# Split fp32r products for q, k and all inputs of the state-space stage in a two-block transformer kernel

## The reference, cut to what matters

```python
proj = x @ w_in                                   # retention: q, k, v, g
q, k, v, g = jnp.split(proj, [RET_QK_W, 2 * RET_QK_W, 2 * RET_QK_W + RET_V_W], axis=-1)
...
prj_c = modulate(rmsnorm(ctx, norm1[layer]), sh1c, sc1c) @ w_in[layer]   # second block: context
prj_l = modulate(rmsnorm(x, norm1[layer]), sh1, sc1) @ w_in[layer]       # second block: tokens
z_c, xbc_c, dt_c, f_c = split_proj(prj_c)
z_l, xbc_l, dt_l, f_l = split_proj(prj_l)
```

## Time and profile before

| what | value |
|---|---|
| time, median of 3 runs | 1798.87 us (1797.41 to 1799.01) |
| span of the profiled execution | 1797.4 us |
| TensorE busy | 1699.7 us (95%) |
| VectorE, ScalarE busy | 642.6 us (36%), 510.6 us (28%) |
| q and k on TensorE | 111.1 to 167.0 us |
| state-space inputs on TensorE | 944.6 to 1096.3 us |

### The profile page before, as it was taken

The page is one execution under the profiler, slowest core; times in us unless marked ns, Lnnn a source line. Parts: engine busy times, 40 slices in busy tenths (PEclk is TensorE's granted clock), DMA queues, the critical chain, the costliest instruction groups (busy, mean ns, idle before and its releaser), DMA issues.

```text
span 1797.4 us, 22709 instructions
## 1 busy us (share of the span) xinstructions
PE 1699.7 (95%) x9752; PEld 1308.8 (73%) x9752; DVE 642.6 (36%) x1038; ACT 510.6 (28%) x751; POOL 5.1 (0%) x13
## 2 busy tenths in 40 slices
PE   6999999999999999999989997869699999999996
PEld 6988899999999989999974476548444545454543
DVE  4434214554365504555323462740321212121212
ACT  5420024444444404444332222430201110111011
POOL 0000000000000000000000000000000000000000
PEclk9999898999899696999969998999799999999999
DMA  9552334555455533555532131002099999999992
GB/s 391 188 187 94 141 141 162 185 186 185 174 190 188 186 140 141 188 188 188 188 140 94 47 141 53 1 4 94 33 396 420 425 416 425 419 424 418 424 419 100
DMA packets 26988, 382.94 MB, mean 213 GB/s; under 512 B 3056, under 2 KB 3184, under 8 KB 3360
## 3 DMA queue, kind: packets, MB, share of 16 engines
q1 hardware_dynamic: 26208, 377.71, 53.7%
q0 software_dynamic: 704, 4.11, 0.6%
HBM read 380.76 MB, written 1.05 MB: 212 GB/s over the span
## 4 chain that ended last, share of the span: by engine, by line
PE 92%; DVE 3%; ACT 3%; issue 1%; DMA 0%; DVEq 0%; ACTq 0%; SPq 0%
PE ps L427 83%; PE ps L770 4%; PE ps L779 4%; DVE HM L1151 1%; ACT HM L839 1%; DVE HM L1139 1%; PE ps L505 1%; ACT work L839 1%; ACT L839 0%; DVE work L1139 0%; PE ps L818 0%; PE ps L812 0%; DMA X<-in_x 0%; ACT SQ L839 0%; DVE work L1151 0%
## 5 line engine op out<-in xcount | busy, mean ns | idle before, releaser
L427 PE MATMUL ps<-ring,work 128*64 128x512 f32 x1536 | 336.9, 595 | 12.3 <-ACT work L839 12.3
L427 PEld LDWEIGHTS ps<-ring,work 128*64 128x64 f32 x1536 | 107.5, 137 | 221.9 <-issue 207.1
L1139 DVE TENSOR_TENSOR w_lo<-ring,w_hi 128x1024 fp32r<-128x1024 f32 x156 | 190.8, 1225 | 191.7 <-ACT w_hi L839 191.2
L427 PE MATMUL ps<-in_hi,w_hi 128*128 128x256 f32 x896 | 256.1, 286 | 0.0
L427 PE MATMUL ps<-in_lo,w_hi 128*128 128x256 f32 x896 | 255.5, 285 | 0.0
L427 PE MATMUL ps<-in_hi,w_lo 128*128 128x256 f32 x896 | 255.2, 285 | 0.0
L839 ACT ACTIVATE work<-ps 128x512 f32<-128x512 f32 (+2 forms) x148 | 87.6, 626 | 575.9 <-PE ps L427 328.9
L839 ACT ACTIVATE w_hi<-ring 128x1024 fp32r<-128x1024 f32 x156 | 164.8, 1058 | 204.5 <-PE ps L427 204.5
L427 PE MATMUL ps<-HM,ring 128*128 128x256 f32 (+1 forms) x704 | 197.7, 441 | 6.8 <-ACT HM L839 6.8
L427 PEld LDWEIGHTS ps<-HM,ring 128*128 128x128 f32 x704 | 133.9, 192 | 63.8 <-issue 49.9
L427 PEld LDWEIGHTS ps<-in_hi,w_hi 128*128 128x128 f32 x896 | 173.1, 193 | 0.0
(11 more groups left out here) (180 smaller groups left out, 1744.6 us busy)
## 6 DMA issues: line engine op xcount, KB each, us to landing
ring<-in_experts SPq DMA_DIRECT2D x96, 2048.0 KB, 12.2
ring<-in_dense SPq DMA_DIRECT2D x83, 2048.0 KB, 8.1
cst<-in_ret_cst POOLq DMA_DIRECT2D x1, 1280.0 KB, 12.8
X<-in_x SPq DMA_DIRECT2D x1, 1024.0 KB, 5.5
cst<-in_ssd_cst POOLq DMA_DIRECT2D x1, 1024.0 KB, 5.0
work<-in_ctx POOLq DMA_DIRECT2D x1, 1024.0 KB, 9.5
out<-HM SPq DMA_DIRECT2D x1, 1024.0 KB, 3.9
cst<-in_wfour POOLq DMA_DIRECT2D x1, 256.0 KB, 2.9
```

The lines of the kernel that those rows point to most:

```text
L427: i = pe.matmul(o, l, r, start=start, stop=stop)
L1139: i = dve.tensor_tensor(out=o, in0=x, in1=y, op=op)
```

## The change

q and k, and all inputs of the state-space stage, become split products with three fp32r passes. dt's weights and the inputs `hcat` are split too (`wdt_hi`, `wdt_lo`, `cat_hi`, `cat_lo`). The 5.5 units of these weights are 44 chunks more, 16 for q and k and 28 for xs, b, c, z and f, which ScalarE copies and VectorE subtracts. To make room, dense units use five slots of the ring, and four in the state-space stage: slot 5 holds two of the three pairs of chunk buffers, slot 4 `cat_hi`. In the state-space stage the third pair lies in `cst`, so that `ssd_cst` is loaded behind f. The experts take the slots in another order.

```diff
+DENSE_SLOTS, SSD_SLOTS = 5, 4
+SLOT = [u % DENSE_SLOTS if u < UNIT_AT["ssd_xs", 0] else (u - UNIT_AT["ssd_xs", 0]) % SSD_SLOTS for u in range(DENSE)]
+TURN = [SLOT[:u].count(SLOT[u]) for u in range(DENSE)]
+EXPERT_SLOT = [2, 4, 5, 3, 0, 1]
...
-        w_at = [("cst", 0), ("work", 2 * KF * T), ("HM", 0)]
+        w_at = [("ring5", 0), ("ring5", 2 * CHUNK), ("HM", 0)]
...
         def chunks_by(name, j):
+            if name == "ssd_in":
+                return min(CHUNK_AT["ssd_xs"][0] + j + 3, CHUNK_AT["ssd_z"][0] + 2)
...
             await_read(pool, TILE["ffn_out1", 3])
+            pool.dma_start(ctxT, a["ctx"]).then_inc(s["ld_ctx"], 16)
+            await_full(pool, TILE["ssd_f", 1])
             pool.dma_start(cst[:, 0:2048], a["ssd_cst"]).then_inc(s["ld_ssd"], 16)
-            pool.dma_start(ctxT, a["ctx"]).then_inc(s["ld_ctx"], 16)
...
-            gemm("ret_q", "q", 8, KD, lambda c: H[:, c, :])
-            gemm("ret_k", "k", 8, KD, lambda c: H[:, c, :])
+            split_gemm("ret_q", KD, KD, in_hi, in_lo, tile="q")
+            split_gemm("ret_k", KD, KD, in_hi, in_lo, tile="k")
...
+            def cat_ready(c):
+                pe.wait_ge(s["cat_lo_ready"], KD + c + 1)
+
             for m in range(KX + KB):
                 name, i = ("ssd_xs", m) if m < KX else ("ssd_b", m - KX)
-                gemm(name, "ssd_in", 1, KD, lambda c: hcat[:, c, :],
-                     (lambda c: pe.wait_ge(s["h_ready"], KD * 5 + c + 1)) if m == 0 else None, cols=2 * T, per=1,
-                     first_block=i * KD, first_tile=m)
+                split_gemm(name, 1, KD, cat_hi, cat_lo, cat_ready if m == 0 else None, tile="ssd_in", per=1, cols=2 * T,
+                           first_tile=m, first_block=i * KD)
...
-            gemm("ssd_z", "ssd_z", KX, KD, lambda c: hcat[:, c, T:2 * T])
-            gemm("ssd_f", "ssd_f", FG, KD, lambda c: hcat[:, c, T:2 * T])
+            split_gemm("ssd_z", KX, KD, lat_hi, lat_lo)
+            split_gemm("ssd_f", FG, KD, lat_hi, lat_lo)
...
+            weights_hi(CHUNK_AT["ffn_in0"][0])
             for j in range(2 * HEADS):
...
             modulated(0, lambda c: hcat[:, c, 0:T], lambda c: coef[:, 0, c:c + 1], lambda c: mod[:, c, 1:2])
+            cat_split(0, 0)
             modulated(1, lambda c: hcat[:, c, T:2 * T], lambda c: coef[:, 1, c:c + 1], lambda c: mod[:, c, 0:1])
+            cat_split(1, T)
+            act.wait_ge(s["ld_wdt"], 16)
+            fn(wdt_hi[:, :, :], wdt[:, :, :], ACT.Copy, s["wdt_hi_ready"])
...
-            weights_lo(CHUNK_AT["ffn_in0"][0])
+            weights_lo(CHUNK_AT["ret_q"][0])
...
             for kind, dst in (("q", q), ("k", k)):
                 for h in range(HEADS):
                     t = TILE[kind, h]
+                    weights_lo(chunks_by(f"ret_{kind}", h))
                     await_full(dve, t)
...
             dve.wait_ge(s["dt_act"], 3)
+            weights_lo(z_chunk + 3)
             log1p_end(dtb, dtc, dta, dtx, scr)
+            weights_lo(z_chunk + 6)
```

More of the change, by code:

```diff
@@ L390, in _ @@
                 with sp.Fori(1, n_rounds) as r:
-                    expert_round(r)
+                    for n in range(RING):
+                        early = 1 if n >= RING - 2 else 0
+                        sp.wait_ge(slot_used[EXPERT_SLOT[n]], r * (EXPERT_UNITS // RING) + (DENSE_USES[EXPERT_SLOT[n]] + early))
+                        load_expert(n, n)
+                    expert_rest(r * (EXPERT_UNITS // RING))
             sp.wait_ge(s["h_ready"], KD * 9)
@@ L869, in inv_rms, with cat_split @@
                 fn(rstd_of(n), lnb[:, :], ACT.Exp, s["rstd_ready"], scale=-0.5)
+            def cat_split(k, lo):
+                for c in range(KD):
+                    act.wait_ge(s["h_ready"], KD * (4 + k) + c + 1)
+                    fn(cat_hi[:, c, lo:lo + T], hcat[:, c, lo:lo + T], ACT.Copy, s["cat_hi_ready"])
             def modulated(k, dst, gain, shift):
@@ L1033, in _ @@
             for m in range(KX + KB):
+                weights_hi(chunks_by("ssd_in", m))
                 padded(m)
@@ L1039, in _ @@
             for m in range(KB):
+                weights_hi(chunks_by("ssd_in", KX + KB + m))
                 padded(KX + KB + m)
@@ L1044, in _ @@
             silu_tile(KX + 2 * KB - 1)
+            weights_hi(CHUNK_AT["ssd_z"][0] + 3)
             act.wait_ge(s["dt_dve"], 1)
@@ L1053, in _ @@
             for j in range(4):
+                weights_hi(chunks_by("ssd_z", j))
                 read(TILE["ssd_z", j], pairs(mix, j), ACT.Silu)
             for j in range(2):
+                weights_hi(chunks_by("ssd_f", j))
                 read(TILE["ssd_f", j], pairs(mix, 4 + j))
@@ L1340, in _ @@
             settle(tt(mod[:, :, :], ps[:, MODB, 0:12 * KD].rearrange("p (a b) -> p a b", b=2), bm, ADD))
-            for n, (chunk, which, gain) in enumerate(((1, 1, "norm1"), (1, 0, "norm1"), (4, 0, "norm2"))):
-                i = stt(coef[:, n, :], mod[:, chunk * KD:(chunk + 1) * KD, which], 1.0, col(gain, 0, KD), ADD, MUL)
+            for n, (sixth, which, gain) in enumerate(((1, 1, "norm1"), (1, 0, "norm1"), (4, 0, "norm2"))):
+                i = stt(coef[:, n, :], mod[:, sixth * KD:(sixth + 1) * KD, which], 1.0, col(gain, 0, KD), ADD, MUL)
             settle(i)
@@ L1346, in _ @@
             normed(9, lambda c: X[:, c, :], lambda c: hcat[:, c, T:2 * T])
+            for of in range(2):
+                for c in range(KD):
+                    part = slice(of * T, (of + 1) * T)
+                    dve.wait_ge(s["cat_hi_ready"], KD * of + c + 1)
+                    tt(cat_lo[:, c, part], hcat[:, c, part], cat_hi[:, c, part].bitcast(F32), SUB, s["cat_lo_ready"])
+            dve.wait_ge(s["wdt_hi_ready"], 1)
+            tt(wdt_lo[:, :, :], wdt[:, :, :], wdt_hi[:, :, :].bitcast(F32), SUB, s["wdt_lo_ready"])
             dve.memset(pad3[:, :, :, 0:CPAD], 0.0)
@@ L1365, in _ @@
             for m in range(KX + KB):
+                weights_lo(chunks_by("ssd_in", m))
                 conv(m)
@@ L1370, in _ @@
             for m in range(KX + KB, KX + 2 * KB):
+                weights_lo(chunks_by("ssd_in", m))
                 conv(m)
+            z_chunk = CHUNK_AT["ssd_z"][0]
             await_read(dve, t)
@@ L1393, in _ @@
                 settle(stt(dst, dtx[:, 0:T], col("backward", rows=ND), dst, MUL, ADD))
+                weights_lo(z_chunk + 8 + 2 * half)
             ts(dtc[:, 0:T], dtc[:, 0:T], stot, SUB, -1.0, MUL, inc=s["dt_dve"])
@@ L1398, in _ @@
             ts(dtx[:, T:2 * T], scr[:, T:2 * T], 1.0, MUL, inc=s["dt_ready"])
+            weights_lo(CHUNK_AT["ssd_f"][0] + CHUNK_AT["ssd_f"][1])
             t = TILE["dt_tok", 0]
```

106 lines of the change are left out of this document (62 added, 44 removed).

## The result

The changed kernel takes 1799.68 us (median of 14 executions, 1798.47 to 1804.44), the kernel before, in the same series, 1793.86 us (14 executions, 1789.87 to 1799.01). The ratio is 1.0033, 95% interval 1.0024 to 1.0042: **slower by 0.33%**, where 0.2% faster was forecast. The first three executions of the kernel before, which stood ahead of the prediction, had the median 1798.87; they are the three slowest of the fourteen.

What follows compares the result with a forecast made beforehand. TensorE was taken as the bound, with 92% of the chain of waits. Gains of 0.7 (q and k) and 3.0 us (up to f's end) made 3.7 off the 1797.4 span: time 1795.2, 0.2% faster, range 1789.5 to 1800.

Steps and rivals of the forecast that it cites:

- At nothing: Ring of five and four slots, earlier expert loads, late ssd_cst load, moved buffers: no wait of TensorE for loads, no cost.
- Behind f all is as before: Everything after the state-space stage's f products: unchanged in length, only shifted as a whole.
- the base of the sum: The profiled execution's span of 1797.4 us, 1.5 below the median 1798.87 of three runs, from which the gain was subtracted.
- q and k: Retention stage: 10.9 us saved by split passes, minus 8.2 idle and 2.0 for the clock; net 0.7 us gained, 0 to 2.
- The start: State-space stage's first product: 11.9 us later, at 956.4, behind ScalarE's rows and copies and VectorE's residuals.
- The wide tiles: Twelve 512-column tiles of the state-space stage: 0.2255 us a pass, a tile every 5.84 us, 1.46 saved on each of eleven.
- The first rival: Wide passes in the state-space stage at 0.2147 us, as fp32 has them: 3.4 us less, 1791.8; chance 0.15.
- z and f: State-space products beside the dt chain: 48.8 us with 11.0 idle and 4.0 for the clock; f ends 3.0 us earlier.
- the second rival: The two later pauses, in z, leave the clock alone: 4.0 us less, 1791.2; chance 0.10.
- longer hand-overs: Longer hand-overs in wide tiles (period 6.1, 2.9 us) or start and dt chain (0.1 a link): 1798 to 1800; chance 0.15.
- The rival with the slow clock in z and f: Clock does not come back in z and f, chunks 19 to 27 take 5.62 us each: +23.3, 1818.5; chance 0.05.

Runs made afterwards that it cites:

- the kernel with the slots alone: Changed kernel with both splits taken back, leaving the ring of five and four slots, early expert loads and late ssd_cst load; 1800.87 us, 1.0050 against the kernel before.

## Why the prediction was wrong, point by point

The steps that failed are "At nothing" (the slots), "Behind f all is as before" (the route stage), and the base of the sum; what the sum gained up to the first state product came out as forecast.

- **q and k: the pause right, the small sum partly by luck.** Forecast 0.7 us gained; q's first product at 119.48 (forecast 119.2) behind 7.28 us of wait (forecast 8.2), the clock at 0.50 from 117.0 to 123.8, and stage A 0.5 and 0.1 us shorter in the two pairs of traces. Two misses of about a microsecond cancel, and both come mostly from v's end, read at 111.1. In the trace of the kernel before, v's last passes start at 111.29 and 111.52, and q and k are

```profile
111.75 55.41 PE L427 MATMUL ps<-HM,ring 128*128 128x256 f32 x256
```

  The window of rows 3 has 261 records, so that the 55.9 us hold a few of v's: q and k take 55.25 us up to the heads, and the split brings 9.9 instead of 10.9. And since v ends later, the pause is shorter.
- **The start: right.** From ScalarE's first modulated row to TensorE's first product 16.5 us, forecast 16.4 (nine of the seventeen copies stand behind the last modulated row, eight ahead of the input's rows). It began 3.2 us earlier (936.7, not 939.9), since B began 0.9 us earlier and took 0.9 less, and the sums met the full clock (1.4), hence 953.2 and not 956.4.
- **The wide tiles: slightly low.** A pass costs 0.229 us, not 0.2255, and a tile comes every 5.94 us, not 5.84: 1.1 us. It is v's end again: the 192 passes of v run from 67.80 to 111.75, 0.229 us each, and the window of rows 3 stops at 111.10, ahead of the last two. The chain of waits has the tiles:

```profile
983.51 5.50 PE ps L454 x24
989.44 5.51 PE ps L454 x24
995.39 5.53 PE ps L454 x24
```

  The first rival, 0.2147 us a pass, is out. The Trainium skill (TensorE: Matmul & The Clock Gate, "Wait — 56ns, not 53.3ns?") gives 215.7 ns for 512 columns at the full clock; a quarter of this kernel's fp32 product agrees (0.859 / 4 = 0.215), its fp32r passes do not, at 0.229.
- **z and f: right in size.** From z's first product (1042.33) to f's end 48.3 us, forecast 48.8; pauses of 5.55, 3.70 and 0.46, forecast 6.1, 4.4 and 0.5. The clock did fall behind the first two, as windows of TensorE show, so the second rival is out:

```profile
1048.00:1054.00 6.00, 0.45 (x3) 0.85 0.21 91
1054.00:1059.00 5.00, 5.00 (x24) 0.50 0.00 0
1059.00:1063.00 4.00, 0.30 (x2) 0.93 0.00 0
1063.00:1066.00 3.00, 3.00 (x15) 0.52 0.02 5
1066.00:1091.00 25.00, 24.54 (x209) 1.00 0.45 168
```

  In sum C and D gained 3.9 us, forecast 3.0; 1.4 of it is that the second sums, with which C begins, met the full clock. Against plain products in the same slots (168.4 and 168.5) the split is worth 2.5.
- **"At nothing": wrong.** The prediction asked of the slots only whether a load would be late, and none was. It did not ask what the slots do to the values that waits compare with. These cost 3.1 us, most of what the state-space stage gains, and the kernel with the slots alone is 6.5 us slower than the kernel before, more than the whole change. About half of the other 3.4 us is the clock that comes back late at the first modulation unit; why it does, and where the rest is, stays open.
- **"Behind f all is as before": wrong.** The route stage took 3.1 us more at 1.2 GHz. No row shown ahead of the prediction gives that stage, but its trace had it: it starts behind an idle stretch, and its clock came back only for a while, so it belonged in the range as a term of its own.
- **The base: wrong.** 1797.4 us was a late execution; against it the parts give +0.2 us (5.7 gained up to the first state product, 3.2 and 3.1 lost, and 0.4 more gained between), while the medians differ by 5.8. The other 5 to 6 us are in that base, most of it in B (733.0 against a typical 728): three executions with 1.6 us between them looked like a narrow base, and 34 of the same kernel in the second series spread from 1790.0 to 1800.8.
- **The rivals.** The time lies just inside the range, on the far side of no change. The rival "longer hand-overs" came near the time by a mechanism that was not there. The rival with the slow clock in z and f is out: the clock was back at 1.00 from 1066 on.

## What to carry to other kernels

Before a change of a ring or its slots is put at nothing, look at every wait value that is computed from them, above all inside loops: two waits of one instruction with different constants are one more register instruction, and behind a semaphore TensorE pays for it each turn (here 0.2 us in each of 16 pairs). A split product on the bound engine gives what its passes promise only where the residual does not stand behind somebody else's chain: put residuals between the links, and keep single instructions there shorter than a chunk lasts (halving the reciprocal took that wait from 3.01 to 0.57 us, and the next one then waited 3.48). And build the sum on stages, not on one execution's span, where the same instructions take 1% more or less by the clock.

## What the runs showed of the hardware

- At the full clock an fp32r pass of 512 columns takes 0.229 us, so that a split product takes 0.687 where the fp32 product takes 0.859; at 256 columns a pass takes 0.118 (45.35 us for 384), the fp32 product 0.432.
- From ScalarE's copy to TensorE's product are 0.69 us where the product itself waits, 0.78 with a semaphore instruction of its own between them, and 0.88 with a register instruction besides.
- One stretch of the same instructions, column B, took 726.6 to 740.2 us in fourteen traces, with TensorE never idle in it and a mean granted clock between 0.92 and 0.90. The route stage took 26.0 to 26.2 us in the seven traces where its transposes began 3.60 to 4.10 us after the clock's fall, and 29.1 to 29.2 in the seven where it was 4.15 to 4.25.
- VectorE's reciprocal of 32x256 takes 1.74 us, of 32x512 3.34: it can be cut to make room between.
